# Block two's pools with the weights before the band matrices, the overflow branch between experts 25 and 26, and the last combine and norm by column halves

## What is computed

```python
y = zeros.at[tok_s].add(y_buf[dest] * w_s)            # combine
x = layer_norm(DN_ALPHA * x + ffn, ln2_g, ln2_b)      # end of block one
h = concatenate([meta, x])                            # 272 rows
a = rmsnorm(h, norm_mix[0])
# pool_mixer: group g of 256 columns, window 2, 4, 8 or 16
outs.append((cs - lag) / cnt - xg)                    # mean of the window less the row
mixed = einsum('blgc,gcd->blgd', pooled, w)           # w: four 256 x 256
h = h + mixed * scale
h = h + swiglu(rmsnorm(h, norm_ffn[0]), w_gate, w_up, w_down)
```

## Time and profile before

| | us |
|---|---|
| median of 3 runs | 1273.5 |
| range | 1272.33 to 1277.43 |
| profiled execution | 1277.75 |
| its span, first to last instruction | 1276.4 |
| PE busy in the span | 1122.0 (88%) |
| DVE, ACT, POOL busy | 589.6, 474.9, 91.5 |
| granted clock of PE, mean | 0.932 |

### The profile page before, as it was taken

The page is one execution under the profiler, slowest core; times in us unless marked ns, Lnnn a source line. Parts: engine busy times, 40 slices in busy tenths (PEclk is TensorE's granted clock), DMA queues, the critical chain, the costliest instruction groups (busy, mean ns, idle before and its releaser), DMA issues.

```text
span 1276.4 us, 22544 instructions
## 1 busy us (share of the span) xinstructions
PE 1122.0 (88%) x9870; PEld 930.3 (73%) x9870; DVE 589.6 (46%) x857; ACT 474.9 (37%) x623; POOL 91.5 (7%) x90
## 2 busy tenths in 40 slices
PE   6999889998776676667776999999999999999998
PEld 6999789864332323333322899999999998999998
DVE  5764567633212221212113576565554447666643
ACT  6544574122111111111114443443346665444442
POOL 0640000000000000000000120000110002100011
PEclk9999899999788878887787899999999999999999
DMA  9833446999999999999999175555553235555530
GB/s 335 261 133 132 141 147 271 423 419 419 421 422 420 421 421 421 421 420 421 415 421 374 60 229 182 163 173 164 183 167 114 84 100 165 174 190 175 173 115 33
DMA packets 146306, 329.37 MB, mean 258 GB/s; under 512 B 6499, under 2 KB 117260, under 8 KB 121631
## 3 DMA queue, kind: packets, MB, share of 16 engines
q1 hardware_dynamic: 143280, 321.47, 66.7%
q10 hardware_dynamic: 2334, 4.35, 1.0%
q0 software_dynamic: 592, 2.10, 0.6%
HBM read 326.83 MB, written 1.06 MB: 257 GB/s over the span
## 4 chain that ended last, share of the span: by engine, by line
PE 60%; DMA 31%; DVE 3%; ACT 2%; issue 2%; POOL 1%; SPq 1%; DVEq 0%; ACTq 0%; POOLq 0%
PE PS L426 14%; PE PS L427 14%; PE PS L428 14%; DMA half<-in_w_down_dram 11%; DMA half<-in_w_gate_up_dram 7%; DMA raw<-in_w_down_dram 6%; DMA spare<-in_w_down_dram 4%; PE PS L745 3%; DMA raw<-in_w_gate_up_dram 2%; PE PS L436 2%; PE PS L437 1%; PE PS L438 1%; PE PS L500 1%; DMA raw<-in_w_in_dram 1%; PE PS L731 1%
## 5 line engine op out<-in xcount | busy, mean ns | idle before, releaser
L1627 DVE TENSOR_TENSOR lo<-raw,hi 128x2048 fp32r<-128x2048 f32 (+1 forms) x114 | 256.7, 2257 | 148.3 <-ACT hi L1190 116.1
L1190 ACT CAST hi<-raw 128x2048 fp32r<-128x2048 f32 (+1 forms) x114 | 211.6, 1858 | 113.2 <-PE PS L428 96.8
L426 PE MATMUL PS<-AH,hi 128*128 128x272 f32 (+1 forms) x832 | 239.1, 287 | 2.6 <-DVE AL L2106 2.2
L428 PE MATMUL PS<-AH,lo 128*128 128x272 f32 (+1 forms) x832 | 238.0, 286 | 0.0
L427 PE MATMUL PS<-AL,hi 128*128 128x272 f32 (+1 forms) x832 | 237.8, 286 | 0.0
L426 PEld LDWEIGHTS PS<-AH,hi 128*128 128x128 f32 x832 | 157.6, 189 | 4.6 <-DVE AL L2106 4.1
L428 PEld LDWEIGHTS PS<-AH,lo 128*128 128x128 f32 x832 | 157.7, 190 | 0.0
L427 PEld LDWEIGHTS PS<-AL,hi 128*128 128x128 f32 x832 | 157.2, 189 | 0.1
L2044 DVE TENSOR_TENSOR Y<-PS,Y 32x256 fp32r<-32x256 f32 x128 | 53.9, 421 | 136.6 <-ACT Y L1385 133.7
L2035 DVE TENSOR_TENSOR T<-T,PS 64x256 f32<-64x256 f32 x32 | 13.5, 423 | 192.3 <-ACT T L1377 192.2
L427 PE MATMUL PS<-FL,hi 128*128 128x272 f32 (+1 forms) x352 | 100.3, 285 | 0.0
(11 more groups left out here) (387 smaller groups left out, 2060.6 us busy)
## 6 DMA issues: line engine op xcount, KB each, us to landing
raw<-in_w_gate_up_dram SPq DMA_DIRECT2D x45, 1024.0 KB, 27.0
spare<-in_w_gate_up_dram SPq DMA_DIRECT2D x43, 1024.0 KB, 27.0
half<-in_w_gate_up_dram SPq DMA_DIRECT2D x40, 1024.0 KB, 27.5
half<-in_w_down_dram SPq DMA_DIRECT2D x23, 1024.0 KB, 27.3
raw<-in_ffn_w_gate_dram SPq DMA_DIRECT2D x22, 1024.0 KB, 5.2
raw<-in_ffn_w_up_dram SPq DMA_DIRECT2D x22, 1024.0 KB, 5.3
raw<-in_w_in_dram SPq DMA_DIRECT2D x21, 1024.0 KB, 8.0
raw<-in_w_down_dram SPq DMA_DIRECT2D x21, 1024.0 KB, 27.5
```

Source lines behind the costliest of these rows:

```text
L426: pe.matmul(o, w(h, c), xh(k), start=start and c == 0, stop=False)
L428: r = pe.matmul(o, w(l, c), xh(k), start=False, stop=stop and c == len(ks) - 1)
L1190: act.copy(K.view(K.hi[i % HN], 0, [[1, n]]), K.view(K.rbuf[i], 0, [[1, n]])).then_inc(S.hi, 1)
L1627: r = e.tensor_tensor(K.view(K.lo[i % HN], 0, [[1, n]]), K.view(K.rbuf[i], 0, [[1, n]]), K.view(K.hi[i % HN], 0, [[1, n]]).bitcast(F32), A ...
```

## The change

Six things are done:

1. **Pools.** pool_w is scaled by the gain (PW, on ACT) and multiplied with the turned, unscaled rows first (units, on PE). ACT scales the result by each token's factor into UR. PE then multiplies UR with the band matrix (mix). XR and PF are gone. The meta rows' part (first_units, UM, first_pools, MM) is done in experts 30 and 31 and ahead of down(31).
2. **Loads.** pool_w has a buffer of its own and is loaded 32 units before the end of the experts. The two copies of the meta rows and the pool matrix are loaded at expert 26.
3. **Overflow.** The flag and its branch stand between experts 25 and 26 on all engines. The experts' functions are called twice, for 0 to 25 and 26 to 31.
4. **Combine and norm.** The last combine goes by column halves, each as soon as its quarters of Y are there. DVE takes the statistics of a half when that half is combined.
5. **Placeholders.** 20 matmuls of Y with itself, in fp32r, in place of 12 fp32 ones; the 4 later ones are gone.
6. **First FFN.** For f=0 PE goes by chunk k over the gate and the up unit together. Gate and up banks are laid out otherwise. The sum of squares (L842, now L884) stands behind the gate unit of f=1, where it stood behind f=0. The two memsets of AH and AL go from DVE to POOL.

```diff
+    K.PW = sb("PW", 2048, A0)
+    K.UR = sb("UR", 2048, A0 + 48 * KB)
+    K.UM = sb("UM", 1024, A0 + 84 * KB, rows=NMETA)
+    K.MTT = sb("MTT", 8 * NMETA, A0 + 46 * KB)
+    K.MM = sb("MM", 16 * NMETA, A0 + 46 * KB + 512)
...
+        elif i == P0:
+            x, name = K.PW, "early5"
+        else:
+            x, name = K.raw[(i - P0 - 1) % RN], f"raw{(i - P0 - 1) % RN}"
...
+    def last_combine():
+        pe.wait_ge(S.pick, 16)
+        for c in range(2):
+            pe.wait_ge(S.y_lo, 4 * NE - 2 + 2 * c)
+            for i in range(2):
+                pe.matmul(bank(2 * i + c, 0, [1, 512]), view(K.SEL, 128 * i, [[1, 128]]), view(K.Y, 512 * c, [[1, 512]]),
+                          start=False, stop=True, skip_group_check=True).then_inc(S.comb, 1)
+    def first_units(h):
+        if h:
+            pe.wait_ge(S.um, h)
+        else:
+            pe.wait_ge(S.lgb, 4)
+            pe.wait_ge(S.hm_t, 16)
+            pe.wait_ge(S.pwn, 8)
+        for g in (2 * h, 2 * h + 1):
+            for c in range(2):
+                r = pe.matmul(bank(PB, 256 * (g % 2), [1, 256], rows=NMETA), view(K.MTT, NMETA * (2 * g + c), [[1, NMETA]]),
+                              view(K.PW, 256 * (2 * g + c), [[1, 256]]), start=c == 0, stop=c == 1)
+        r.then_inc(S.um_pe, 1)
+    def first_pools():
+        pe.wait_ge(S.um, 2)
+        pe.wait_ge(S.pm, 16)
+        for k in range(8):
+            r = pe.matmul(bank(PB, 2 * NMETA * k, [1, 2 * NMETA]), view(K.UM, 128 * k, [[1, 128]], rows=NMETA),
+                          K.pm(4 * BANDW + 2 * NMETA * (k // 2), 2 * NMETA, NMETA), start=True, stop=True)
+        r.then_inc(S.pe_step, 1)
...
+        elif e >= NE - 2:
+            first_units(e - (NE - 2))
+    if e1 == NE:
+        first_pools()
+        down(NE - 1)
+        last_combine()
...
+            pe.wait_ge(S.ht, NE)
+            pe.wait_ge(S.warm, 3)
         for k in range(8):
-            r = pe.transpose(bank(2 * i, 128 * k, [1, 128]), view(K.X1, 1024 * i + 128 * k, [[1, 128]]), con("ident"))
...
+            r = pe.transpose(bank(4, 128 * k, [1, 128]), view(K.X1, 1024 * i + 128 * k, [[1, 128]]), con("ident"))
+            if k % 4 == 3:
+                r.then_inc(S.xt_pe, 1)
+    def units(i):
+        b = 0 if i else 6
+        if i:
+            pe.wait_ge(S.x1_dve, 3)
+        else:
+            pe.wait_ge(S.y_lo, 4 * NE)
+            pe.wait_ge(S.dve_step, STEP["meta"])
+        for g in range(4):
+            if g % 2 == 0:
+                pe.wait_ge(S.xt_act, 4 + 2 * i + g // 2)
+            for c in range(2):
+                k = 2 * g + c
+                r = pe.matmul(bank(b, 256 * g, [1, 256]), view(K.HH, L * k + NMETA + 128 * i, [[1, 128]]), view(K.PW, 256 * k, [[1, 256]]),
+                              start=c == 0, stop=c == 1)
+            if g == 1:
+                r.then_inc(S.u_pe, 1)
+        r.then_inc(S.unit if i else S.u_pe, 1)
+    def mix(i):
+        w = 128 if i else 128 + NMETA
+        if i:
+            pe.wait_ge(S.ur, 4)
+        else:
+            pe.wait_ge(S.ur, 2)
+            pe.wait_ge(S.x1_dve, 4)
+            pe.wait_ge(S.pm, 16)
+        for k in range(8):
+            r = pe.matmul(bank(mix_bank(k), 256 * (k % 2) + 128 * i, [1, w]), view(K.UR, 1024 * i + 128 * k, [[1, 128]]), pm(BANDW * (k // 2), w),
+                          start=i == 0 and k % 2 == 0, stop=i == 1, skip_group_check=True)
+            if i and k % 2:
+                r.then_inc(S.mixed, 1)
     pe.wait_ge(S.ht, NE)
-    pe_warm(pe, K, S, 12, 5)
+    for n in range(20):
+        r = pe.matmul(bank(4, 0, [1, 256]), view(K.Y, 0, [[1, 128]]), view(K.Y, 0, [[1, 256]]), start=True, stop=True)
+    r.then_inc(S.warm, 1)
     turn(0)
...
+    units(0)
     turn(1)
...
-        for m in range(2):
-            k = 2 * g + m
...
-            for c in range(2):
-                r = pe.matmul(bank(k % 4, 0, [1, L]), view(K.rbuf[K.P0], 256 * (2 * g + c) + 128 * m, [[1, 128]]), hc(K.PF, 2 * g + c),
-                              start=c == 0, stop=c == 1)
-            if k < 7:
-                r.then_inc(S.pw, 1)
-            else:
-                r.then_inc(S.unit, 1)
+    mix(0)
+    units(1)
+    mix(1)
...
+        if f == 0 and i == 0:
+            for n in units:
+                lo_done(pe, K, S, n)
+            for k in range(8):
+                normed(k)
+                for which in range(2):
+                    for m in range(2):
+                        if k == 0:
+                            bank_free(f, b(which, m))
+                        r = stationary(pe, K, units[which], bank(b(which, m), 0, [1, w]), m, (k,), xh, xl, start=k == 0, stop=k == 7, c0=k)
+                    if k == 7:
+                        r.then_inc(S.unit, 1)
+            continue
+        for which, n in enumerate(units):
             lo_done(pe, K, S, n)
             for m in range(2):
...
+                if m == 0 or f < 2:
+                    bank_free(f, b(which, m))
+                if f == 1 and b(which, m) == 7:
                     pe.wait_ge(S.rs_dve, 6 if i else 1)
-                r = stationary(pe, K, n, bank(b, 0, [1, w]), m, range(8), lambda k: tc(K.AH, k, q0), lambda k: tc(K.AL, k, q0),
-                               before=normed if f == 0 and which == 0 and m == 0 else None)
+                r = stationary(pe, K, n, bank(b(which, m), 0, [1, w]), m, range(8), xh, xl, before=normed if f == 0 and which == 0 and m == 0 else None)
             r.then_inc(S.unit, 1)
-        if f == 0:
...
-            pe_factors(pe, K, S, ni, 7, q0)
+            if which == i and f == 1 - i:
+                norm_sums()
...
+    def first_units(h):
+        act.wait_ge(S.um_pe, h + 1)
+        act.activation(view(K.UM, 512 * h, [[1, 512]], rows=NMETA), bank(PB, 0, [1, 512], rows=NMETA), ACT.Copy,
+                       scale=view(K.small, 83, [[1, 1]], rows=NMETA)).then_inc(S.um, 1)
...
+        for n in range(2):
+            act.wait_ge(S.xt_pe, 4 + 2 * i + n)
+            act.copy(view(K.HH, L * 4 * n + NMETA + 128 * i, [[L, 4], [1, 128]]), bank(4 + n, 0, [128, 4], [1, 128])).then_inc(S.xt_act, 1)
+    def units(i, n):
+        if i and n:
+            act.wait_ge(S.unit, K.P0 + 1)
+        else:
+            act.wait_ge(S.u_pe, 2 * i + n + 1)
+        act.activation(view(K.UR, 1024 * i + 512 * n, [[1, 512]]), bank((0 if i else 6) + n, 0, [1, 512]), ACT.Copy, scale=K.sm(85 + 2 * i)).then_inc(S.ur, 1)
     round_hi(act, K, S, K.P0 + 1)
     act_sqrt_row(act, K, S, 0, 3)
+    turned(0)
+    act.wait_ge(S.x1_dve, 3)
+    act_squares(act, K, S, 2, rows(0))
+    act_sqrt_row(act, K, S, 1, 4)
     round_hi(act, K, S, K.P0 + 2)
-    act.wait_ge(S.x1_dve, 3)
-    act_squares(act, K, S, 2, x1(0))
-    act_scaled(act, K, S, 1, K.MT[:, :], K.XRM[:, :])
-    act_sqrt_row(act, K, S, 1, 4)
-    act_scaled(act, K, S, 2, x1(0), xr(0))
-    turned(0)
+    act_root(act, K, S, 2)
+    for n in range(2):
+        units(0, n)
+    turned(1)
     act.wait_ge(S.x1_dve, 4)
-    act_squares(act, K, S, 3, x1(1))
-    act_scaled(act, K, S, 3, x1(1), xr(1))
-    turned(1)
+    act_squares(act, K, S, 3, rows(1))
+    act_root(act, K, S, 3)
     for n in range(2):
-        act.wait_ge(S.pl_pe, 4 + n)
-        for k in (4 + 2 * n, 5 + 2 * n):
-            r = act.activation(view(K.PF, L * k + NMETA, [[1, 256]]), bank(6 + n, 256 * (k % 2), [1, 256]), ACT.Copy, scale=par("nm", k))
-        r.then_inc(S.pl_act, 1)
-    for g in range(4):
-        if g == 3:
-            act.wait_ge(S.unit, K.P0 + 1)
-        else:
-            act.wait_ge(S.pw, 2 * g + 2)
-        for k in (2 * g, 2 * g + 1):
-            act_chunk(act, K, S, 0, k, par("nf", k), 0)
+        units(1, n)
+    for k in range(8):
+        act_chunk(act, K, S, 0, k, par("nf", k), 0)
...
+    def norm(i, between=None):
+        o, x = view(K.X1, 1024 * i, [[1, 1024]]), bank(2 * i, 0, [1, 1024])
+        for c in range(2):
+            dve.wait_ge(S.comb, 31 + i + 2 * c)
+            r = dve.bn_stats(st(i, 6 * c, 6), bank(2 * i + c, 0, [1, 512]))
+        a = own(r)
+        own.wait(dve, a)
+        a = own(dve.bn_aggr(st(i, 12, 2), st(i, 0, 12)))
+        own.wait(dve, a)
+        a = own(dve.tensor_scalar(st(i, 14), st(i, 13), 1e-5, None, ALU.add))
+        own.wait(dve, a)
+        dve.reciprocal(st(i, 14), st(i, 14)).then_inc(S.ln_rec, 1)
+        a = own(dve.scalar_tensor_tensor(o, x, st(i, 12), gain, ALU.subtract, ALU.mult))
+        if between is not None:
+            between()
+        own.wait(dve, a)
+        dve.wait_ge(S.ln_sqrt, 3 + i)
+        dve.scalar_tensor_tensor(o, o, st(i, 14), offset, ALU.mult, ALU.add).then_inc(S.x1_dve, 1)
...
+    norm(0)
+    norm(1, lambda: factor(2))
+    rest_lo(dve, K, S, K.P0 + 1)
+    rest_lo(dve, K, S, K.P0 + 2)
+    dve.wait_ge(S.u_pe, 2)
+    near = view(K.HH, NMETA, [[L, 8], [1, NMETA]])
+    dve.tensor_tensor(near, near, view(K.MM, NMETA, [[2 * NMETA, 8], [1, NMETA]]), ALU.add).then_inc(S.dve_step, 1)
     factor(3)
```

(26 more changed lines are left out.)

373 lines of the change are left out of this document (158 added, 215 removed).

## The result

| us | before | after |
|---|---|---|
| median | 1274.35 (7 runs, 1272.33 to 1277.59) | 1268.87 (7 runs, 1267.72 to 1269.47) |
| profiled execution | 1277.75 | 1268.95 |
| its span | 1276.4 | 1267.6 |
| its mean granted clock | 0.932 | 0.928 |

The ratio is 0.9947, with a 95% interval of 0.9933 to 0.9962. It is the ratio of the means, 1275.3 and 1268.6, which lie 6.7 us apart. Between the medians lie 5.5 us, and 8.8 between the two profiled executions, because the profiled one of before is among its slowest. The forecast was 1265.3 with a range of 1257.5 to 1271.5: the time lies in the range, 3.6 us above the forecast. The sum of terms was -8.2.

The account below looks back on a forecast made before the run. Bounds: DMA while expert weights stream, PE from about 748 us, a chain of small dependent steps between. Terms +3.0 + 2.2 - 1.9 - 18.1 + 6.6 = -8.2 against the median 1273.5 give 1265.3 us, range 1257.5 to 1271.5.

Parts of the forecast that it names:

- Part 1: Expert stage: loading pool_w before the last 32 expert units puts one megabyte more in the saturated queue, +3.0 us.
- Part 2: Between turn(31) and down(31): PE's work for the 16 meta rows delays down(31), +2.2 us, bounds +0.6 and +4.1.
- Its lower bound, +0.6: The smallest cost the prediction allowed for the meta rows' work ahead of down(31), in us.
- Part 3: Last Y to x1(0): combine and norm by halves, no branch and no table load on the way, -1.9 us.
- Part 4: From x1(0) to the end of f=0 in block two: 45.7 us become 27.6, -18.1.
- Of these 7.0 are the fetch and the placeholders: Share of the 18.1 us gained up to the end of f=0, put down to the branch's instruction fetch and the placeholders.
- the trace agrees with its 5.34 us: Claim that PE's idle behind the branch matches the skill's stall: a taken branch outside the window forces a DMA fetch.
- Rival C: The tail stays slow: the 5.34 us idle is PE's own after any such code change, 1270.6 us; 28% with its other form.
- C's other form: The clock is at half from the combine to units(0), about 1269 us; shares the 28%.
- Part 5: End of f=0 to f=2: the later sum of squares makes PE wait 4.8 us, then half clock 1.8; +6.6 us.
- rival D: Before expert 26, PE's instruction fetch outlasts the 27 us of cover; 1292 us if it takes 54; 6%.
- the 39 that were worked out from whole packets: Fetch time in us amid the expert stream if DMA engines drain whole packets per ring, seven times 5.34; whole 1277.

Follow-up runs that it names:

- pool_load_twice: The changed kernel with the megabyte of pool weights loaded a second time into a free region, ACT waiting for it behind the experts; 1271.62 us.
- branch_at_end: The changed kernel with the overflow flag and branch put back between the experts and block two; 1270.09 us.
- before_shifted: The kernel before, jump kept, with 64 more PE instructions (waits met long ago) that move it in the code; 1270.6 us, ratio 0.9957 to before.
- end_shifted190: The changed kernel with the overflow part back between experts and block two, plus 190 PE instructions of waits long met; 1276.41 us, ratio 1.0005 to before.
- split_ahead: The changed kernel with ACT's and DVE's copies of f=2's gate weights moved ahead of the root and silu of f=0; 1262.58 us.
- sums_after_f0: The changed kernel with the sum of squares put back right behind the gate unit f=0; 1264.47 us.
- after_no_branch: The changed kernel without the overflow part (no test, no jump); 1269.23 us.
- before_no_branch: The kernel before without the overflow part (flag test, jump and the code behind it left out); 1270.13 us.
- meta_late: The changed kernel with first_pools moved from ahead of down(31) to behind the last combine, in place of 12 placeholders; 1267.85 us.

## Why the prediction was right, and where not

Each term, from the marks of the two profiled executions:

| part | forecast | measured | from |
|---|---|---|---|
| 1 pool weights in the stage | +3.0 | +2.9 | last landing but two 686.0 to 688.9 |
| 2 meta rows before down(31) | +2.2 | +1.4 | last Y 695.59 to 699.92, less 2.9 |
| 3 combine and norm by halves | -1.9 | -1.7 | last Y to x1(0), 6.43 to 4.72 |
| 4 x1(0) to the end of f=0 | -18.1 | -18.2 | 45.7 to 732.1 - 704.64 = 27.5 |
| 5 end of f=0 to f=2 | +6.6 | +6.7 | 12.3 to 17.2 + 1.8 |
| sum | -8.2 | -8.9 | executions: -8.8 |

The end of f=0 in the trace after is taken where the first matmul of f=1 starts, 732.11: L884 starts at 738.16, behind 48 matmuls of 0.126. f=2 starts at 749.33 and runs at half clock to 753.8, 18 matmuls, each 0.1 us longer than at full clock, which costs 1.8.

**Part 1** is confirmed twice, by the landing and by pool_load_twice.

**Part 2** was right in its chain (down(31) was to start at 694.8 and starts at 694.88), and 0.8 too dear in its last step: down(31) was given 3.0 to 3.9 us, and took 2.76, because more of it ran at full clock (0.96 at 694 to 696). Its lower bound, +0.6, doesn't follow from its own steps, which give 1.5 at the least (694.8 + 3.0 against 696.3); the measured 1.4 lies below that.

**Part 3** holds. Its reason, the table loads, is what branch_at_end brought back: 0.7 us between the last Y and x1(0), and 1.2 in the whole.

**Part 4** holds in its size: from x1(0) to the start of f=0 15.3 us for the 15.6 forecast, and f=0 itself 12.1 for 12.0. It fails in one reason. "Of these 7.0 are the fetch and the placeholders": the idle follows a jump, but a jump at this place does not bring it by itself. With the overflow part back in its old place the new kernel lost 1.2, and not 5 or 6. The step that failed is that I took the idle of one program as the price of every jump there, and moving the jump as what takes it away. It is the price of a jump at the seam whose target stands just before the border of a block, which 64 instructions elsewhere also take away (before_shifted) and 190 bring back (end_shifted190). The reading had the sign in its own rows: I wrote that two placeholder records ran behind the branch, where the earlier trace rows shows one, and that a record ran at all means that the target was there; what came late was code behind it. So "the trace agrees with its 5.34 us" was said too quickly. That the size came right is in part luck: without the jump at the seam there can be none of this idle, but with the jump left there the new code would have been free of it too, by its place alone.

Rival C had the 5.34 as "PE's own after any such change of code". The changed kernel has no jump at the seam and no idle; end_shifted190, with the same order of work and the jump back, has both, so C was not far off, and my 28% for it had no count of instructions behind it, which could have been made before. C's other form, half clock from the combine to units(0), had the number nearest to the measured one, about 1269, but it didn't happen: the granted clock is 1.00 from 704 us on, and turn(0) and units(0) took 1.09 and 3.69.

**Part 5** is right in place, releaser and size: 4.8 us of wait forecast, 4.50 measured, lo of f=2 as the releaser, half clock behind it. Of the two experiments that take it away split_ahead gained 6.3 of the 6.6, and sums_after_f0 4.4, with waits of 1.0 for POOL and 0.2 for lo in its place. In both profiled executions f=0 starts 0.6 to 0.7 later than in the changed kernel's (720.61 and 720.67 against 719.98), which these edits don't touch; with it the terms close to within half a us.

**The fetch in the saturated stage** (rival D, with 27 us of cover) didn't show: after_no_branch gives no difference. PE's queue of instructions has a packet at 599 to 600 us in the changed kernel and one at 605 to 606, 4 and 10 us after the flag's load (595.2), and none from 594 to 608 in after_no_branch. So a fetch for the jump seems to come through the stream of weights well within D's 27 us, and far from the 39 that were worked out from whole packets. How long PE would have to wait for it there was not measured, as the target stands far before a border.

**The 3.6 us between forecast and median.** The sum was right to 0.6 for the profiled executions, and applied to a median 4.25 us below the profiled one of before. The medians differ by 5.5 and not 8.8: the executions of before scatter (25 runs of it, made beside the later experiments, had a median of 1275.96, between 1273.93 and 1280.32), and those of the changed kernel don't. What in before scatters was not found, but for the stretch at half clock in f=0, worth 1.8, that some executions have and some don't; the changed kernel's f=0 ran at 1.00 throughout. The runs of before_shifted and before_no_branch, which don't have the idle, lie within 2.8 us, but end_shifted190 has it and lies within 1.4, so it isn't the idle alone.

**What the change is worth beside the idle.** With the idle taken out of before by shifting its code, 1270.6, the changed kernel's 1268.87 is only 1.7 better, or 1.4 by after_no_branch, which was measured beside it. By the two traces the new order wins 6.7 us between turn(0) and f=0 (703.42 to 725.45 in before_shifted, 704.70 to 719.98 after) and 3.9 in f=0 (16.0 to 12.1), and gives back 1.3 before turn(0) and 6.7 at f=2. So about 4 of the 5.5 us are the loss of an idle that 64 instructions elsewhere take away as well.

## What to carry to other kernels

Idle time that no row of the profile explains, a few instructions behind a taken jump, can be a matter of where the code stands: add some dozens of instructions that do nothing, in a stage that waits for something else, before you ascribe it to the jump or to the work around it, and before you credit a change with its loss. Look at the granted clock of both executions too before you read a difference of 2 us. When a reduction is moved to a later unit, look up what its result holds back on every engine in program order: here the copies of the next weights stood behind it, and moving these (6.3 us) was worth more than moving the sum back (4.4). And let the sum of a forecast start from several executions, not from the one that was profiled.

## What was new about the chip

- After a jump that passes over 305 instructions, PE ran on at once in the block of the target, and stood at that block's end until 7.2 to 7.3 us after the load of the flag (695.7 to 702.93, 695.6 to 702.78, 694.5 to 701.80, 700.2 to 707.37), whether one record or nine had run in between. The Trainium skill (Runtime: NRT & Kernel Launch, Instruction fetch mechanics) tells of a stall when the target isn't in the window of two pages. In these four traces the target itself was there (by the count it lies in the block behind the jump's own), and the block behind it was not. A reading that fits: the fetch of a block begins when the one ahead of it is entered, and a jump to a block's last instructions leaves it no time. A packet of 16 KB falls 4.3 to 5.0 us after the flag's load in all four (in end_shifted190 between 704.5 and 705.0), and 2.3 to 2.9 before PE goes on; that they are what PE waits for, and when they were asked for, is not shown.
- The same 16 records of 16x32 took 1.97 us at full clock before down(31), and 3.62 in meta_late behind the combine, where the granted clock was 0.50 from 698 us on, after PE's wait for Y.
- Some executions of one order of work have a stretch of 3.5 us at half clock in f=0 and others don't, behind the same two waits of about 1.06 and 0.28 us.
